# Three classical pairs instead of four ahead of the Strassen pairs in both feed-forwards, with the roles of two buffer sets exchanged and another order of work at the hand-over

## The chip, the cores and the metric

One core of a Trainium2 chip runs the whole kernel. The metric is the device time of one execution in microseconds; lower is better.

## The reference

Two layers of an encoder on x of shape (1, 512, 1024), all in float32. Layer 0 mixes tokens with gated linear attention, layer 1 with chunked softmax attention; behind each mixer stands a residual LayerNorm, then a SwiGLU feed-forward and a second residual LayerNorm. The change touches only the feed-forward, which runs once in each layer:

```python
FFN_HIDDEN = -(-8 * D_MODEL // (3 * 256)) * 256        # 2816
def swiglu(x, w_in, w_out):
    gate, up = jnp.split(x @ w_in, 2, axis=-1)
    return (jax.nn.silu(gate) * up) @ w_out
...
        h = layer_norm(DEEPNORM_ALPHA * h + swiglu(h, ffn_w_in[i], ffn_w_out[i]), ln_g[i, 1], ln_b[i, 1])
```

## The kernel before

Every large product is made in three TensorE matmuls: both operands are held as a high part (rounded to fp32r by ScalarE, "hi") and the rest (made by VectorE or GpSimd as value minus high part, "lo"), and `three` adds hi x hi, hi x lo and lo x hi in PSUM. Weights come as a stream of slabs of 128 x 1024, two to a DMA, into two raw buffers (`raw`). Each raw buffer is loaded again when both parts of its two slabs are made (the wait of SyncE before `load_pair`).

The hidden width of 2816 is 22 chunks of 128 columns. A chunk takes a pair of slabs, one of gate and one of up weights. The first four pairs (`PLAIN = 4`) are classical: 8 blocks of 128 rows for gate and for up, all 512 tokens, 48 matmuls of 512 columns (in pairs 0 and 1 the tokens are taken in two halves, because the LayerNorm ahead delivers them so). Behind them, 18 pairs (`FAST`) are made by a Strassen scheme: gate weights over up weights times early over late tokens is a 2 x 2 block product, made in 7 half-size products of 12 matmuls of 256 columns each instead of 8. `pair` of TensorE has them in order: product 1 (a11), 2 (s3), 3 (s2), 4 (a12), 5 (s1), 6 (a22), 7 (s4). Products 1, 3, 5 and 7 are added in one bank, `out_a`, whose state ScalarE copies out on the way: `copy_p1` behind product 1, `copy_u2` behind 3, `copy_u4` behind 5, `gate_late` behind 7. TensorE may begin product 3 only after `copy_p1`, 5 only after `copy_u2`, 7 only after `copy_u4`.

What the other engines do for pair (i, j), which is Strassen pair 2i + j, in program order on each in-order engine:

- VectorE, one pair ahead: the sums of weights `sums_31` and `sums_24`, and the low parts `form_plain_low`, `form_s32_low`, `form_s1_low`, `form_s4_low`. Behind the products it adds banks to the copies (`gate_of_early`, `u3`, `up_of_late`, `up_of_early`) and multiplies gate by up (`hidden_early`, `hidden_late`).
- ScalarE, one pair ahead: the high parts `form_plain_high`, `form_s32_high`, `form_s1_high`, `form_a22_high`, `form_s4_high`; then the copies and the two Silu (`gate_early`, `gate_late`).
- GpSimd: the low parts of classical slabs (`split_lo`), and of one block of each Strassen pair (`form_a22_low`, 128 x 512), which it starts when its high part is there.

Sums of x are needed once for a feed-forward: `sum_x` makes t1, t2, t3 and t4; ScalarE and VectorE split them. The split of t4 is written over tokens that classical products read, so it waits for the last of these. Its VectorE half (line 1316, "split of t4" below) stands in the queue of VectorE ahead of all forms of pair (0, 1), and its ScalarE half (line 679) ahead of the copies of pair (0, 0). Product 6 of the first pair waits for it.

In the head of a feed-forward, `plain_prod(c)` of VectorE multiplies Silu of gate (`gate(c)` of ScalarE) by the bank of up for classical pair c. `w_s32`, `w_s4` are two sets of buffers for the weight sums, `gate_s` and `prod` hold the copies, two halves each.

Of the kernel before, what the change touches and what calls it, by code (L numbers as in the profile page):

```python
# [82 lines left out]
PLAIN = 4  # L83
# [24 lines left out]
def build_program(nc, a):  # L108
    ctx = ExitStack()
    with ctx:  # L110
# [89 lines left out]
        def halves_at(name, shape, hi, lo):  # L200
# [6 lines left out]
        w_s32 = [halves_at("w_s32_0", [P, 2, HALF], region + 76 * KB, region + 44 * KB),  # L207
                 halves_at("w_s32_1", [P, 2, HALF], region + 68 * KB, gb_at)]
        w_s4 = [halves_at("w_s4_0", [P, HALF], region + 80 * KB, region + 82 * KB),
                halves_at("w_s4_1", [P, HALF], region + 72 * KB, region + 74 * KB)]  # L210
# [198 lines left out]
        def blocks_of(n0, j):  # L409

            slot = (n0 + 2 * j) % RING
            return slot, slot + 1, (n0 // 2 + j) % RAWS
# [59 lines left out]
        def _(act):  # L472
# [94 lines left out]
            def feed_forward(f, n0):  # L567
                banks = SUM_BANKS[f]

                def gate(c):  # L570
                    act.wait_ge(slab_done, n0 + 2 * c + 1)
                    if c >= 2:
                        act.wait_ge(prod_done[f], c - 1)
                    nc.scalar.activation(gate_s[:, c % 2, :], bank[GATE_BANKS[f][c % 2]][:, :], ACT.Silu).then_inc(silu_done[f], 1)
# [109 lines left out]
                with act.Fori(2, FAST // 2 - 1) as i:  # L684
                    pair(i, 0, False, False)
                    pair(i, 1, False, False)
                pair(FAST // 2 - 1, 0, False, False)
                pair(FAST // 2 - 1, 1, False, False, True)
                hidden_high(f, 2)
                gate_late(FAST // 2 - 1, 1, False)  # L690
# [262 lines left out]
        def _(pool):  # L953
# [30 lines left out]
            def feed_forward(f, n0):  # L984
# [93 lines left out]
        def _(dve):  # L1078
# [80 lines left out]
            def sum_x(f, ln):  # L1159
# [31 lines left out]
            def feed_forward(f, n0):  # L1191
                banks = SUM_BANKS[f]

                def plain_prod(c):
                    dve.wait_ge(slab_done, n0 + 2 * c + 2)
                    dve.wait_ge(silu_done[f], c + 1)
                    nc.vector.tensor_tensor(act_a[:, c, :], gate_s[:, c % 2, :], bank[UP_BANKS[f][c % 2]][:, :],
# [77 lines left out]
                def pair(i, j, begun, last=False):  # L1275
# [31 lines left out]
                plain_prod(2)  # L1307
# [6 lines left out]
                plain_prod(3)  # L1314
# [3 lines left out]
                pair(0, 0, False)  # L1318
                pair(0, 1, True)
                with dve.Fori(1, FAST // 2 - 1) as i:  # L1320
                    pair(i, 0, True)
                    pair(i, 1, True)
                pair(FAST // 2 - 1, 0, True)
                pair(FAST // 2 - 1, 1, True, True)
                up_of_late(FAST // 2 - 1, 1)
                up_of_early(FAST // 2 - 1, 1)
                hidden_early(FAST // 2 - 1, 1)
                hidden_low(f, 2)
                hidden_late(FAST // 2 - 1, 1)
# [272 lines left out]
        def _(pe):  # L1602
# [121 lines left out]
            def feed_forward(f, n0, ln):  # L1724
# [14 lines left out]
                for c in range(RING):  # L1739
# [415 lines left out]
```

## Time and profile before

| what | value |
|---|---|
| median of 3 runs | 1172.85 us (1171.49 to 1173.0) |
| the profiled execution's own time | 1171.48 us |
| its span | 1169.8 us |
| PE busy | 1154.0 us, 99% of the span |
| DVE / ACT / POOL busy | 696.7 / 528.0 / 419.9 us |
| share of the chain that ended last on PE | 93% |

The profile is one execution. PE is TensorE's matmuls, DVE is VectorE, ACT is ScalarE, POOL is GpSimd. In a timeline, a row has the start in us from the start of the span, the duration in us, engine, line, operation, output and inputs. In square brackets stands how long the engine was idle before it and what ended that; a row without brackets followed on its predecessor, or nearly. Durations of neighbours overlap a little, since an engine issues the next instruction before the last is drained, so the cost of an instruction in a full queue is the distance of two starts.

### The profile page before, as it was taken

To read this page: it belongs to the slowest core of one execution; us is meant where nothing else is said; L and a number is where in the kernel's file an instruction comes from. 1 tells how busy PE (TensorE), PEld (TensorE's weight loads), DVE (VectorE), ACT (ScalarE), POOL (GpSimd) and SP (SyncE) were. 2 spreads that over 40 slices of the span, in tenths; PEclk is the share of its full clock that TensorE was granted. 3 is DMA by queue.
4 is the path that set the end of the run, shared out by engine and by line. 5 is a ranking of instruction groups with operands and counts; after the bars stand their busy time and mean duration, and the time that the engine had idled before them with its cause. 6 is when DMAs were issued, how large, how long until landed. Compare 5 with 4: busy or idle time off the path is not lost.

```text
span 1169.8 us, 18906 instructions
## 1 busy us (share of the span) xinstructions
PE 1154.0 (99%) x6958; PEld 1019.0 (87%) x6958; DVE 696.7 (60%) x1173; ACT 528.0 (45%) x918; POOL 419.9 (36%) x247
## 2 busy tenths in 40 slices
PE   8999999999999999999999999999999999999997
PEld 6887888989999998888887777778999999998885
DVE  4070163788888874443504676736888888854435
ACT  4345244245555554332415666662455555553222
POOL 2538426041111115446245343472311111144441
PEclk9999999999999999999999999999999999999999
DMA  6433314142233333325032212142223333333211
GB/s 219 154 152 108 108 37 144 49 149 97 104 108 108 108 108 144 107 74 180 19 108 73 90 46 90 46 145 72 69 76 109 108 108 108 108 120 121 84 72 72
DMA packets 21976, 119.89 MB, mean 102 GB/s; under 512 B 2448, under 2 KB 6672, under 8 KB 8992
## 3 DMA queue, kind: packets, MB, share of 16 engines
q1 hardware_dynamic: 15440, 104.96, 25.5%
q10 hardware_dynamic: 6480, 14.17, 3.5%
q8 instruction: 37, 0.61, 0.2%
q14 instruction: 19, 0.16, 0.0%
HBM read 117.02 MB, written 5.24 MB: 105 GB/s over the span
## 4 chain that ended last, share of the span: by engine, by line
PE 93%; DVE 3%; ACT 2%; POOL 1%; DMA 1%; issue 1%; ACTq 0%; DVEq 0%; POOLq 0%
PE bank L1605 28%; PE bank L1607 28%; PE bank L1606 28%; PE bank L1996 2%; PE bank L1981 2%; PE bank L1667 1%; DVE s_g_c L1384 1%; DMA s_x_t<-x_t 1%; PE bank L2017 1%; PE bank L2016 1%; PE bank L1865 1%; PE bank L1858 0%; PE bank L1873 0%; POOL s_g_rg L1026 0%; POOL s_w_lo L970 0%
## 5 line engine op out<-in xcount | busy, mean ns | idle before, releaser
L970 POOL TENSOR_TENSOR s_w_lo<-s_raw,s_w_hi 128x1024 fp32r<-128x1024 f32 x108 | 266.3, 2476 | 307.5 <-ACT s_w_hi L497 307.5
L1605 PE MATMUL bank<-s_t_hi,s_w_hi 128*128 128x256 f32 (+1 forms) x832 | 265.4, 319 | 0.7 <-POOL s_w_lo L970 0.7
L1607 PE MATMUL bank<-s_t_hi,s_w_lo 128*128 128x256 f32 (+1 forms) x832 | 263.1, 316 | 0.0
L1606 PE MATMUL bank<-s_t_lo,s_w_hi 128*128 128x256 f32 (+1 forms) x832 | 262.7, 316 | 0.0
L497 ACT ACTIVATE s_w_hi<-s_raw 128x1024 fp32r<-128x1024 f32 x111 | 116.3, 1059 | 225.0 <-PE bank L1607 200.2
L989 POOL TENSOR_TENSOR s_w_lo<-s_raw,s_w_hi 128x512 fp32r<-128x512 f32 x36 | 64.3, 1785 | 305.1 <-ACT s_w_hi L597 305.1
L1607 PEld LDWEIGHTS bank<-s_t_hi,s_w_lo 128*128 128x128 f32 x832 | 158.6, 191 | 10.6
L1605 PEld LDWEIGHTS bank<-s_t_hi,s_w_hi 128*128 128x128 f32 x832 | 158.7, 191 | 10.2 <-POOL s_w_lo L970 1.1
L1606 PEld LDWEIGHTS bank<-s_t_lo,s_w_hi 128*128 128x128 f32 x832 | 158.8, 191 | 9.3
L1188 DVE TENSOR_TENSOR s_a_lo<-s_act_a,s_a_hi 128x512 fp32r<-128x512 f32 x44 | 84.7, 1938 | 108.7 <-ACT s_a_hi L565 108.5
L1605 PE MATMUL bank<-s_w_hi,s_a_hi 128*128 128x512 f32 x352 | 137.2, 390 | 0.0
L1606 PE MATMUL bank<-s_w_lo,s_a_hi 128*128 128x512 f32 x352 | 137.0, 389 | 0.0
L1607 PE MATMUL bank<-s_w_hi,s_a_lo 128*128 128x512 f32 x352 | 137.0, 389 | 0.0
L1605 PE MATMUL bank<-s_t_hi,s_w_s_hi 128*128 128x256 f32 x432 | 122.4, 283 | 0.0
L1607 PE MATMUL bank<-s_t_hi,s_w_s_lo 128*128 128x256 f32 x432 | 122.3, 283 | 0.0
L1606 PE MATMUL bank<-s_t_lo,s_w_s_hi 128*128 128x256 f32 x432 | 122.2, 283 | 0.0
L1605 PE MATMUL bank<-s_w_hi,s_t_hi 128*128 128x512 f32 x288 | 113.9, 395 | 3.3 <-DVE s_t_lo L1350 1.4
L1607 PE MATMUL bank<-s_w_hi,s_t_lo 128*128 128x512 f32 x288 | 112.3, 390 | 0.0
L1606 PE MATMUL bank<-s_w_lo,s_t_hi 128*128 128x512 f32 x288 | 112.1, 389 | 0.0
L1605 PEld LDWEIGHTS bank<-s_t_hi,s_w_s_hi 128*128 128x128 f32 x432 | 82.9, 192 | 0.1
L1606 PEld LDWEIGHTS bank<-s_t_lo,s_w_s_hi 128*128 128x128 f32 x432 | 82.9, 192 | 0.0
L1607 PEld LDWEIGHTS bank<-s_t_hi,s_w_s_lo 128*128 128x128 f32 x432 | 82.9, 192 | 0.0
(200 smaller groups left out, 2052.8 us busy)
## 6 DMA issues: line engine op xcount, KB each, us to landing
s_raw<-stream SPq DMA_DIRECT2D x97, 1024.0 KB, 4.7
s_ln_gb<-ln_gb ACTq DMA_DIRECT2D x4, 1024.0 KB, 5.9
bias_rows<-rel_bias ACTq DMA_DIRECT2D x1, 3072.0 KB, 12.7
s_h<-x ACTq DMA_DIRECT2D x1, 2048.0 KB, 12.5
s_r_b<-bias_rows ACTq DMA_DIRECT2D x16, 128.0 KB, 2.4
s_x_t<-x_t ACTq DMA_DIRECT2D x3, 512.0 KB, 12.5
out<-s_h SPq DMA_DIRECT2D x3, 512.0 KB, 2.6
s_x_t<-x_t ACTq DMA_DIRECT2D x2, 256.0 KB, 5.8
```

The lines of the kernel that those rows point to most:

```text
L497: nc.scalar.activation(w_parts(n, slice(0, SLAB))[0], raw[:, pair % RAWS, n % 2, :], ACT.Copy).then_inc(hi_done, 2 if n == 1 else 1)
L970: nc.gpsimd.tensor_tensor(lo, raw[:, place // 2 % RAWS, n % 2, :], hi.bitcast(F32), ALU.subtract).then_inc(lo_done, 2 if n == 1 else 1)
L989: nc.gpsimd.tensor_tensor(w_lo[:, up_at, HALF:], raw[:, slot, 1, HALF:], w_hi[:, up_at, HALF:].bitcast(F32), ALU.subtract).then_inc(lo_don ...
L1188: nc.vector.tensor_tensor(a_lo[:, k, :], act_a[:, k, :], a_hi[k % HI_RING][:, :].bitcast(F32), ALU.subtract).then_inc(a_lo_done[f], 1)
L1384: nc.vector.tensor_tensor_scan(g_c[:, hd, :], keep[:, :], g_c[:, hd, :], 0.0, ALU.mult, ALU.add).then_inc(cum_done, 1)
L1605: nc.tensor.matmul(out, l_hi, r_hi, start=start, stop=False, skip_group_check=skip)
L1606: nc.tensor.matmul(out, l_hi, r_lo, start=False, stop=False, skip_group_check=skip)
L1607: return nc.tensor.matmul(out, l_lo, r_hi, start=False, stop=stop, skip_group_check=skip)
L1667: last = nc.tensor.transpose(bank[banks[t][half]][:, k * P:(k + 1) * P], src[:, t, (4 * half + k) * P:(4 * half + k + 1) * P], ident[:, :])
L1865: last = nc.tensor.matmul(bank[GLA_O_BANKS[t][hd // 2]][:, (hd % 2) * GLA_DV:(hd % 2 + 1) * GLA_DV], g_am[:, t % 2, hd * P:(hd + 1) * P], ...
L1981: last = nc.tensor.matmul(bank[2 + hd][:, keys], qk[q][rows, toks], qk[k][rows, keys], start=(i == 0), stop=(i == 2))
L1996: last = nc.tensor.transpose(bank[4 + hd][:, at * P:(at + 1) * P], r_p[:, s % 4, j * P:(j + 1) * P], ident[:, :])
```

## The change

`PLAIN` goes from 4 to 3, and `FAST` so from 18 to 19: nine iterations of two pairs and one more pair, (9, 0), at the end, which is now the last with j = 0. The classical pair that goes is one of the two made whole (48 matmuls of 512 columns). The two sets of `w_s32` and `w_s4` exchange their places, and the classical gates use the two halves of `gate_s` in the other order. On VectorE the second half of t4's sum becomes `add_x4` and moves from ahead of `plain_prod(0)` to behind the forms of pair (0, 0); `plain_prod(2)` is the last classical product. The first Strassen pair gets functions of its own: on ScalarE `copy_p1` and then the split of t4, on VectorE the sums of pair (0, 1) first, then `gate_of_early`, `u3`, and `up_of_late` between the low parts.

The comments that name an engine are added here.

```diff
-PLAIN = 4
+PLAIN = 3
...
-        w_s32 = [halves_at("w_s32_0", [P, 2, HALF], region + 76 * KB, region + 44 * KB),
-                 halves_at("w_s32_1", [P, 2, HALF], region + 68 * KB, gb_at)]
+        w_s32 = [halves_at("w_s32_0", [P, 2, HALF], region + 68 * KB, gb_at),
+                 halves_at("w_s32_1", [P, 2, HALF], region + 76 * KB, region + 44 * KB)]
...
-            slot = (n0 + 2 * j) % RING
-            return slot, slot + 1, (n0 // 2 + j) % RAWS
+            slot = (n0 + 2 * (PLAIN + j)) % RING
+            return slot, slot + 1, (n0 // 2 + PLAIN + j) % RAWS
...
                 def pair(i, j, start, before_start, last=False):     # ScalarE
                     i_next, j_next = (i, 1) if j == 0 else (i + 1, 0)
-                    if before_start is not None:
-                        gate_late(i if j else i - 1, 1 - j, before_start)
+                    gate_late(i if j else i - 1, 1 - j, before_start)
...
-                    if before_start is None:
-                        copy_u2(i, j)
                     form_s32_high(i_next, j_next)
                     form_s1_high(i_next, j_next)
                     form_a22_high(i_next, j_next)
-                    if before_start is not None:
-                        copy_u2(i, j)
+                    copy_u2(i, j)
                     form_s4_high(i_next, j_next)
                     gate_early(i, j)
                     copy_u4(i, j, start)
+
+                def first_pair():                                    # ScalarE
+                    copy_p1(0, 0, True)
+                    act.wait_ge(slab_done, n0 + 2 * PLAIN)
+                    act.wait_ge(x_summed[f], 4)
+                    nc.scalar.activation(t_hi[:, 0:KD // 2, LATE_TOKS], t4_sum[:, :, :], ACT.Copy).then_inc(x_sum_hi[f], 1)
+                    copy_u2(0, 0)
+                    form_plain_high(0, 1)
+                    copy_u4(0, 0, True)
+                    form_s32_high(0, 1)
+                    form_s1_high(0, 1)
+                    form_a22_high(0, 1)
+                    form_s4_high(0, 1)
+                    gate_early(0, 0)
 
                 gate(0)
                 split_hi(n0 + RING)
                 split_hi(n0 + RING + 1)
                 x_sums_high()
                 gate(1)
-                split_hi(n0 + RING + 2)
-                split_hi(n0 + RING + 3)
-                gate(2)
                 form_plain_high(0, 0)
...
                 form_s4_high(0, 0)
-                gate(3)
-                act.wait_ge(slab_done, n0 + 2 * PLAIN)
-                act.wait_ge(x_summed[f], 4)
-                nc.scalar.activation(t_hi[:, 0:KD // 2, LATE_TOKS], t4_sum[:, :, :], ACT.Copy).then_inc(x_sum_hi[f], 1)
-                pair(0, 0, True, None)
+                gate(2)
+                first_pair()
                 pair(0, 1, True, True)
...
+                def first_pair():                                    # VectorE
+                    sums_31(0, 1)
+                    sums_24(0, 1)
+                    gate_of_early(0, 0)
+                    u3(0, 0)
+                    form_plain_low(0, 1)
+                    up_of_late(0, 0)
+                    form_s32_low(0, 1)
+                    form_s1_low(0, 1)
+                    form_s4_low(0, 1)
...
                 plain_prod(1)
-                plain_prod(2)
                 sums_31(0, 0)
                 sums_24(0, 0)
                 form_plain_low(0, 0)
                 form_s32_low(0, 0)
                 form_s1_low(0, 0)
                 form_s4_low(0, 0)
-                plain_prod(3)
+                add_x4(f)
+                plain_prod(2)
                 dve.wait_ge(x_sum_hi[f], 4)
                 nc.vector.tensor_tensor(t_lo[:, 0:KD // 2, LATE_TOKS], t4_sum[:, :, :], t_hi[:, 0:KD // 2, LATE_TOKS].bitcast(F32),
                                         ALU.subtract).then_inc(x_sum_lo[f], 1)
-                pair(0, 0, False)
-                pair(0, 1, True)
+                first_pair()
+                pair(0, 1, late_made=True)
...
-                for c in range(RING):                                # TensorE
+                for c in range(2 * PLAIN - RING):
                     pe.wait_ge(lo_done, n0 + RING + c + 1)
...
                 with pe.Fori(1, FAST // 2) as i:
                     pair(i, 0, False)
                     pair(i, 1, False)
+                pair(FAST // 2, 0, False)
```

With `late_made`, VectorE's `pair` leaves out its `up_of_late`, which `first_pair` has made. GpSimd gets one `form_a22_low` more behind its loop and two `split_lo` fewer in each head.

## Rows read from the trace of the kernel before

**Rows 1.** The page, part 1: busy time and share of the span by engine.
```profile
PE 1154.0 (99%) x6958; PEld 1019.0 (87%) x6958; DVE 696.7 (60%) x1173; ACT 528.0 (45%) x918; POOL 419.9 (36%) x247
```

**Rows 2.** Waits of PE over the whole run: total, times, longest (us).
```profile
PE bank L1605 <- DVE s_t_lo L1350: 1.4, 1, 1.4
```

**Rows 3.** Timeline of PE: start, duration, instruction; the head of feed-forward 0.
```profile
242.38 0.40 PE L1605 MATMUL bank<-s_t_hi,s_w_hi 128*128 128x512 f32 x1
...
264.17 0.28 PE L1605 MATMUL bank<-s_t_hi,s_w_hi 128*128 128x256 f32 x1
...
274.31 0.28 PE L1605 MATMUL bank<-s_t_hi,s_w_hi 128*128 128x256 f32 x1
...
280.07 0.28 PE L1605 MATMUL bank<-s_t_hi,s_w_hi 128*128 128x256 f32 x1
...
284.39 0.28 PE L1605 MATMUL bank<-s_t_hi,s_w_hi 128*128 128x256 f32 x1
```

**Rows 4.** Timeline of DVE, same head; 862.00 is the second head.
```profile
241.90 3.31 DVE L1181 TENSOR_TENSOR s_t_sum<-s_t_sum,s_t_lo 128x1024 f32<-128x1024 f32 x1
...
254.09 0.69 DVE L1204 TENSOR_TENSOR s_w_s_sum<-s_raw 128x512 f32<-128x512 f32 x1
...
257.88 1.22 DVE L1227 TENSOR_TENSOR s_w_s_lo<-s_w_s_sum,s_w_s_hi 128x1024 fp32r<-128x1024 f32 x1
...
259.02 1.79 DVE L1233 TENSOR_TENSOR s_w_lo<-s_s_sum,s_w_hi 128x512 fp32r<-128x512 f32 x1
...
260.73 0.68 DVE L1238 TENSOR_TENSOR s_w_s_lo<-s_w_s_sum,s_w_s_hi 128x512 fp32r<-128x512 f32 x1
...
265.46 1.22 DVE L1316 TENSOR_TENSOR s_t_lo<-s_t_sum,s_t_hi 128x1024 fp32r<-128x1024 f32 x1 [0.41 <-ACT s_t_hi L679]
...
272.19 1.12 DVE L1233 TENSOR_TENSOR s_w_lo<-s_s_sum,s_w_hi 128x512 fp32r<-128x512 f32 x1
...
273.24 0.68 DVE L1238 TENSOR_TENSOR s_w_s_lo<-s_w_s_sum,s_w_s_hi 128x512 fp32r<-128x512 f32 x1
...
276.57 0.68 DVE L1212 TENSOR_TENSOR s_w_s_sum<-s_s_sum,s_raw 128x512 f32<-128x512 f32 x1
...
862.00 1.23 DVE L1316 TENSOR_TENSOR s_t_lo<-s_t_sum,s_t_hi 128x1024 fp32r<-128x1024 f32 x1 [0.41 <-ACT s_t_hi L679]
```

**Rows 5.** The page, part 6: loads of weights; count, KB each, median us to landing.
```profile
s_raw<-stream SPq DMA_DIRECT2D x97, 1024.0 KB, 4.7
```

**Rows 6.** Timeline of ACT, same head.
```profile
256.14 1.06 ACT L589 ACTIVATE s_w_s_hi<-s_w_s_sum 128x1024 fp32r<-128x1024 f32 x1 [1.23 <-DVE s_w_s_sum L1212]
...
264.37 1.06 ACT L679 ACTIVATE s_t_hi<-s_t_sum 128x1024 fp32r<-128x1024 f32 x1 [4.84 <-PE bank L1607]
...
268.68 0.38 ACT L613 ACTIVATE s_gate_s<-bank 128x256 f32<-128x256 f32 x1 [2.04 <-PE bank L1607]
...
277.28 1.06 ACT L589 ACTIVATE s_w_s_hi<-s_w_s_sum 128x1024 fp32r<-128x1024 f32 x1 [0.95 <-DVE s_w_s_sum L1212]
...
279.29 0.36 ACT L613 ACTIVATE s_gate_s<-bank 128x256 f32<-128x256 f32 x1
...
279.55 0.62 ACT L601 ACTIVATE s_w_s_hi<-s_w_s_sum 128x512 fp32r<-128x512 f32 x1
```

**Rows 7.** Timeline of POOL, same head: what it writes for the first two Strassen pairs.
```profile
258.37 1.88 POOL L989 TENSOR_TENSOR s_w_lo<-s_raw,s_w_hi 128x512 fp32r<-128x512 f32 x1 [10.90 <-ACT s_w_hi L597]
...
271.18 1.59 POOL L989 TENSOR_TENSOR s_w_lo<-s_raw,s_w_hi 128x512 fp32r<-128x512 f32 x1 [10.92 <-ACT s_w_hi L597]
```

**Rows 8.** Timeline of DVE and PE where PE waits for line 1350.
```profile
13.30 1.22 DVE L1350 TENSOR_TENSOR s_t_lo<-s_x_t,s_t_hi 128x1024 fp32r<-128x1024 f32 x1 [0.29 <-ACT s_t_hi L715]
...
14.98 0.39 PE L1606 MATMUL bank<-s_w_lo,s_t_hi 128*128 128x512 f32 x1
```

**Rows 9.** Windows: length, then busy us of PE, PEld, DVE, ACT, POOL; a later pair.
```profile
284.40:294.50 10.10, 10.10 (x87) 10.10 (x86) 8.32 (x14) 5.48 (x10) 1.80 (x1) 1.00 0.36 127
```

**Rows 10.** The page, part 2: granted TensorE clock in 40 slices, in tenths.
```profile
PEclk9999999999999999999999999999999999999999
```

More of the change, by code:

```diff
@@ L573, in gate @@
                         act.wait_ge(prod_done[f], c - 1)
-                    nc.scalar.activation(gate_s[:, c % 2, :], bank[GATE_BANKS[f][c % 2]][:, :], ACT.Silu).then_inc(silu_done[f], 1)
+                    nc.scalar.activation(gate_s[:, (c + 1) % 2, :], bank[GATE_BANKS[f][c % 2]][:, :], ACT.Silu).then_inc(silu_done[f], 1)
                 def x_sums_high():
@@ L683, in feed_forward @@
                 pair(1, 1, False, False)
-                with act.Fori(2, FAST // 2 - 1) as i:
+                with act.Fori(2, FAST // 2) as i:
                     pair(i, 0, False, False)
                     pair(i, 1, False, False)
-                pair(FAST // 2 - 1, 0, False, False)
-                pair(FAST // 2 - 1, 1, False, False, True)
+                pair(FAST // 2, 0, False, False, True)
                 hidden_high(f, 2)
-                gate_late(FAST // 2 - 1, 1, False)
+                gate_late(FAST // 2, 0, False)
                 for k in range(3, HI_RING):
@@ L998, in feed_forward @@
                     form_a22_low(i, 1)
+                form_a22_low(FAST // 2, 0)
                 for n in range(n0 + 2 * KF, n0 + 2 * KF + RING):
@@ L1180, in sum_x, with add_x4 @@
                 own(nc.vector.tensor_tensor(t4_sum[:, :, :], t_hi[:, KD // 2:, EARLY_TOKS].bitcast(F32), t2[:, :, :], ALU.subtract))
+            def add_x4(f):
                 nc.vector.tensor_tensor(t4_sum[:, :, :], t4_sum[:, :, :], t_lo[:, KD // 2:, EARLY_TOKS].bitcast(F32),
                                         ALU.add).then_inc(x_summed[f], 1)
-                dve.wait_ge(x_summed[f], 4)
             def hidden_low(f, k):
@@ L1196, in plain_prod @@
                     dve.wait_ge(silu_done[f], c + 1)
-                    nc.vector.tensor_tensor(act_a[:, c, :], gate_s[:, c % 2, :], bank[UP_BANKS[f][c % 2]][:, :],
+                    nc.vector.tensor_tensor(act_a[:, c, :], gate_s[:, (c + 1) % 2, :], bank[UP_BANKS[f][c % 2]][:, :],
                                             ALU.mult).then_inc(prod_done[f], 1)
@@ L1273, in hidden_late, with pair @@
                     hidden(i, j, LATE_TOKS, prod[:, bass.ds(j, 1), LATE_TOKS], prod[:, bass.ds(j, 1), EARLY_TOKS], 2)
-                def pair(i, j, begun, last=False):
+                def first_pair():
[8 more added lines that the diff above has]
+                    form_s4_low(0, 1)
+                def pair(i, j, late_made=False, last=False):
                     i_next, j_next = (i, 1) if j == 0 else (i + 1, 0)
                     i_old, j_old = (i, 0) if j == 1 else (i - 1, 1)
-                    if begun:
+                    if not late_made:
                         up_of_late(i_old, j_old)
-                        up_of_early(i_old, j_old)
-                        hidden_early(i_old, j_old)
+                    up_of_early(i_old, j_old)
+                    hidden_early(i_old, j_old)
                     if not last:
                         sums_31(i_next, j_next)
-                    if begun:
-                        hidden_late(i_old, j_old)
+                    hidden_late(i_old, j_old)
                     if last:
@@ L1317, in feed_forward @@
                                         ALU.subtract).then_inc(x_sum_lo[f], 1)
-                pair(0, 0, False)
-                pair(0, 1, True)
[L1320 to L1327, printed above, removed]
+                first_pair()
+                pair(0, 1, late_made=True)
+                with dve.Fori(1, FAST // 2) as i:
+                    pair(i, 0)
+                    pair(i, 1)
+                pair(FAST // 2, 0, last=True)
+                up_of_late(FAST // 2, 0)
+                up_of_early(FAST // 2, 0)
+                hidden_early(FAST // 2, 0)
                 hidden_low(f, 2)
-                hidden_late(FAST // 2 - 1, 1)
+                hidden_late(FAST // 2, 0)
                 for k in range(3, KF):
```

4 lines of the change are left out of this document (2 added, 2 removed).

## The prediction

> **What bounds the kernel now.** I read the shares first. TensorE is busy for 99% of the span [rows 1], no other engine for more than 60%. Then its waits: behind the first matmuls the longest is 1.4 us, at 13 us of the span [rows 2], and none lies in a feed-forward. Then the starts of its matmuls in the head of feed-forward 0 [rows 3]: from 242.38 to 264.17 lie 96 matmuls of 512 columns, (264.17 - 242.38) / 96 = 0.227 us each; from 274.31 to 284.39 the 84 of a Strassen pair, 0.120 us each. Both stretches are free of gaps. So the time is TensorE's queue, and a change is worth what it takes out of that queue less the gaps that it opens. The second head repeats the first: line 1316 runs there at 862.00 after the same idle time of 0.41 as at 265.46 [rows 4]. All terms below count twice.
>
> **What goes out of TensorE's queue.** A classical pair of 48 x 0.227 = 10.90 us is replaced by one more Strassen pair of 84 x 0.120 = 10.08 us [rows 3]. That is -0.82 us per head, -1.64 us in all. The first Strassen pair keeps its 10.14 us (274.31 - 264.17). If nothing waits, this is the whole effect.
>
> **Are the forms of pair (0, 0) there in time?** Let T be the start of product 1 of pair (0, 0); it was 264.17 and becomes 242.38 + 10.90 = 253.28. There is still one classical pair to cover the forms. `add_x4` leaves the front of VectorE, so `plain_prod(0)` starts where line 1181 did, at 241.90. With 1.14 for a 1024-wide instruction (257.88 to 259.02) and 0.6 for a 512-wide one (half of it and the overhead; line 1238 lasts 0.68 with the overlap) [rows 4], the sums begin at 241.90 + 0.6 + 3 x 1.14 + 0.6 = 246.5, the low part of s32 ends 257.88 + 1.22 - 254.09 = 5.0 us later at 251.5, and s4's issue is over at 246.5 + (260.73 + 0.6 - 254.09) = 253.8, T + 0.5. Products 1 and 2 need only the parts up to s32: 1.8 us to spare at T. s1 and s4 are needed at T + 5.8 and T + 8.6. `add_x4` is then over at about T + 0.5 + 1.2 = T + 1.7. So no gap here; I price it at 0, and from the other side at 0.5 us, should the three low parts of the x sums run slower than 1.14.
> The two `split_lo` that go from GpSimd, the exchanged buffers and the halves of `gate_s` change no wait that is last: the buffers' former readers are classical slabs or the LayerNorm, done before 242.38. GpSimd's part of pair (0, 0) ends 1.15 behind the low part of s32, as before (260.25 against 259.10), so at 252.7, T - 0.6; it was T - 3.9. Only then is the raw buffer of pair (1, 0) loaded: 4.7 us [rows 5], landed at T + 4.3 and first wanted at T + 10. Price 0; 0.3 if a load took twice that.
>
> **The split of t4 moves to the back of the first copy.** Before, ScalarE began it at 264.37, T + 0.20 [rows 6], and VectorE's half followed at 265.46, T + 1.29 [rows 4]. Now `copy_p1` stands ahead of it. `copy_u2` in the same pair began at 268.68, ended by a wait for PE [rows 6]: three products are 36 x 0.120 = 4.32, so the answer to PE takes 0.19. `copy_p1` so starts at T + 1.44 + 0.19 = T + 1.63, the next instruction 0.26 later (279.29 to 279.55) [rows 6]: t4's ScalarE half starts at T + 1.89, VectorE's half at T + 1.89 + 1.09 = T + 3.0. VectorE is 1.7 us later than before at this point, and everything that forms pair (0, 1) and begins pair (1, 0) is behind it in the queue. Between 265.46 and 276.57 no row of VectorE has idle time ahead of it to make this up [rows 4].
>
> **What is late next.** I follow the same instructions with their distances of before. `s1_low` of pair (0, 1) was at 272.19, 6.73 behind the split [rows 4]; one `up_of_late` (256 columns, 0.33 by the 512-wide ones) is put ahead of it: T + 10.06, with `s32_low` 1.14 ahead at T + 8.92. GpSimd: `copy_u4` starts at T + 7.20 + 0.19, the high parts follow at T + 7.65, and `form_a22_low` is ready to start 258.37 - 256.14 = 2.23 after that, T + 9.88 [rows 6, 7]. That is inside `s32_low`, just as in pair (0, 0) of before (257.88, 258.37, 259.02): there GpSimd ended 1.15 us after `s32_low` (260.25 against 259.10), `s1_low` ended 0.56 us after GpSimd, and it cost 260.73 - 259.02 = 1.71 us instead of 0.6 [rows 4, 7]. For pair (0, 1) before, two additions from PSUM lay between, and it cost 1.05. They are now ahead of the low parts, so I take 1.71: `s4_low` at T + 11.77, where it was at T + 9.07. `up_of_late` is done already (-0.33), so from here VectorE is 2.37 us late.
> The Trainium skill, page SBUF — State Buffer, section "Who interferes with whom", says that a VectorE instruction with two SBUF inputs and a GpSimd instruction that reads SBUF exclude each other, and that the later one waits for the whole of the first. By that rule `s1_low` would run its full 0.68 behind GpSimd's end; the rows have 0.56 and 0.54. The sum would be 0.1 us larger per head.
> `sums_24` of pair (1, 0) was at 276.57, T + 12.40, and comes at T + 14.77. ScalarE's high part of s32 follows 0.71 later (277.28), T + 15.48, and `copy_u2` of pair (0, 1) is queued behind that and two more high parts: 279.29 - 277.28 = 2.01 later, T + 17.49, ending at T + 17.85 [rows 4, 6]. Behind this copy waits product 5 of pair (0, 1). It started at 280.07 = T + 15.90 [rows 3], when the copy had ended at 279.65, 0.42 us before. After a wait TensorE takes up its pace 14.98 - 0.227 - (13.30 + 1.22) = 0.23 us behind the release [rows 8]: T + 18.08. The gap is 18.08 - 15.90 = 2.2 us.
> Bounds of this gap: with a lag of 0.4 in place of 0.19 at each of the two answers of ScalarE to PE in the chain, 2.6. If GpSimd gets in only after `s1_low`, the extra 0.66 is not paid: 1.5. Below that only if the queue is not as I read it: 0.
> Behind it the delay ends. VectorE needs 8.32 of the 10.1 us of a pair [rows 9], and the gap itself gives it 2.2 us. `copy_u4` of (0, 1), queued behind `form_s4_high` and `gate_early`, is wanted at T + 21.0 and can start at T + 19.7; the first low part of (1, 0) ends near T + 17.4, wanted at T + 22.4. The last pair with j = 0 instead of 1 has the same instructions and waits: 0, or at most a few tenths.
>
> **Sum.** Per head -0.82 + 2.2 = +1.4, twice +2.8 us. The profiled execution becomes 1171.48 + 2.8 = 1174.3; its 1171.48 lies 1.37 under the median of the runs, so I put the same sum on the median: 1172.85 + 2.8 = 1175.6 us, +0.24%.
>
> **Rivals.**
> (1) No gap; the order with the copies first holds TensorE, and only the queue's saving is left: -1.64, 1171.2. For it: the copy had 0.42 to spare, and ScalarE is idle much of the time. Against it: the 1.7 us are larger than this, and VectorE's queue had no idle time between the two points. It decides if VectorE's lag at `sums_24` of (1, 0) stays under 0.2 us. This is the not-slower side.
> (2) The gap without the collision: 1.5 per head, +1.4 in all, 1174.2. GpSimd's start at T + 9.88 is only 0.2 ahead of the end of `s32_low`; a few tenths would turn the order.
> (3) A second gap per head, of about 1 us, because `form_a22_low` or the first forms come late as well: +4.8, 1177.6. Against it: the spare times above.
> (4) The gap lets the clock fall. It would be longer than any wait since 13 us, and the granted clock stands at full in all slices [rows 10]. At 1.2 instead of 2.4 GHz the 36 matmuls left in the pair would cost 4.3 us more, 8.6 in all: 1184.
> The Trainium skill, page TensorE: Matmul & The Clock Gate, section "HAM oscillation — how this bites in real kernels", says that idle gaps between matmuls can halve the clock. No wait here did that; 1.4 us did not.
>
> **How the numbers follow.** The forecast has 0.50, rival (1) 0.15, (2) 0.18, (3) 0.13, (4) 0.04. A measurement of this kernel can tell about 0.2%, 2.35 us, from no change. Slower by more: most of the forecast (0.37; its own range is 1174.6 to 1176.5), (3) and (4): 0.53. Same: the rest of the forecast, (2) and nearly all of (1): 0.43. Faster: 0.04, since -1.64 is within the bound. The range of 1171.0 to 1177.8 holds all but (4) and a little of the others' spread; the runs of before alone spread over 1.5 us.
>
> **What would show it.** Right: one wait of TensorE of about 2.2 us in each head, in front of product 5 of pair (0, 1), released by ScalarE's copy at line 613; that copy behind three high parts; the split of t4 at T + 3.0 on VectorE; `s1_low` of pair (0, 1) of 1.7 us beside a GpSimd row; 10.08 us for each later pair. Wrong: no such wait, or one at T, T + 7.2 or in pair (1, 0), or a granted clock under full.

## The result and the profile after

| | median of all runs | lowest to highest | runs |
|---|---|---|---|
| before | 1171.49 us | 1171.02 to 1173.0 | 6 |
| after | 1176.17 us | 1174.57 to 1178.21 | 6 |

The ratio is 1.0035, with a 95% interval of 1.0025 to 1.0046: the change makes the kernel 4.7 us slower. The forecast of +2.8 us, a ratio of 1.0024, lies just below this interval; the forecast of the time, 1175.6 us, is 0.6 us off. The profiled execution of after took 1175.38 us, 3.90 more than that of before, with a span of 1173.7 us. The functions moved down by 17 lines in `three` (L1605 to L1607 became L1622 to L1624), line 1316 is now 1334, 1227 is 1234, 1233 is 1240, 1238 is 1245, 1212 is 1219, 679 is 664.

The page of after, part 1, against [rows 1]: 72 more matmuls are recorded (each pair exchanged turns 48 into 84), and TensorE's busy time is 1.2 us less, though the span is longer. What came on top is waiting.

```profile
PE 1152.8 (98%) x7030; PEld 1020.9 (87%) x7030; DVE 706.1 (60%) x1199; ACT 533.6 (45%) x932; POOL 410.8 (35%) x245
```

The longest of TensorE's waits in after, with total, times and longest:

```profile
PE bank L1622 <- ACT s_gate_s L613: 4.0, 2, 2.0
```

This is a wait that before did not have: twice 2.0 us, released by ScalarE's copy at line 613. The timeline of TensorE in head 0 of after answers to [rows 3]:

```profile
243.35 0.40 PE L1622 MATMUL bank<-s_t_hi,s_w_hi 128*128 128x512 f32 x1
...
254.25 0.28 PE L1622 MATMUL bank<-s_t_hi,s_w_hi 128*128 128x256 f32 x1
...
264.33 0.28 PE L1622 MATMUL bank<-s_t_hi,s_w_hi 128*128 128x256 f32 x1
...
269.97 0.28 PE L1624 MATMUL bank<-s_t_hi,s_w_lo 128*128 128x256 f32 x1
272.26 0.36 PE L1622 MATMUL bank<-s_t_hi,s_w_hi 128*128 128x256 f32 x1 [2.01 <-ACT s_gate_s L613]
...
276.65 0.28 PE L1622 MATMUL bank<-s_t_hi,s_w_hi 128*128 128x256 f32 x1
...
286.73 0.28 PE L1622 MATMUL bank<-s_t_hi,s_w_hi 128*128 128x256 f32 x1
```

Three stretches are to be read. Classical pair to T: 254.25 - 243.35 = 10.90. Pair (0, 0): 10.08. Pair (0, 1): 276.65 - 264.33 = 12.32 in place of 10.08; behind its product 4 TensorE starts nothing for 272.26 - 269.97 = 2.29 us, 2.17 more than its pace. Pair (1, 0): 10.08 again. The second feed-forward shows the same at 868.07. From the first of these classical matmuls to the end of the last pair a feed-forward took 203.29 us before (242.38 to 445.67, and 838.92 to 1042.21) and takes 204.66 and 204.65 now (to 448.01 and 1046.10): 1.36 us more each.

The other engines in the same head, T = 254.25; VectorE, against [rows 4]:

```profile
257.25 1.23 DVE L1334 TENSOR_TENSOR s_t_lo<-s_t_sum,s_t_hi 128x1024 fp32r<-128x1024 f32 x1 [0.72 <-ACT s_t_hi L664]
...
263.18 1.22 DVE L1234 TENSOR_TENSOR s_w_s_lo<-s_w_s_sum,s_w_s_hi 128x1024 fp32r<-128x1024 f32 x1
264.31 1.79 DVE L1240 TENSOR_TENSOR s_w_lo<-s_s_sum,s_w_hi 128x512 fp32r<-128x512 f32 x1
266.03 0.68 DVE L1245 TENSOR_TENSOR s_w_s_lo<-s_w_s_sum,s_w_s_hi 128x512 fp32r<-128x512 f32 x1
...
269.03 0.69 DVE L1219 TENSOR_TENSOR s_w_s_sum<-s_s_sum,s_raw 128x512 f32<-128x512 f32 x1
```

ScalarE, against [rows 6]:

```profile
255.89 0.38 ACT L609 ACTIVATE s_gate_s<-bank 128x256 f32<-128x256 f32 x1 [3.25 <-PE bank L1624]
256.17 1.05 ACT L664 ACTIVATE s_t_hi<-s_t_sum 128x1024 fp32r<-128x1024 f32 x1
...
269.75 1.06 ACT L589 ACTIVATE s_w_s_hi<-s_w_s_sum 128x1024 fp32r<-128x1024 f32 x1 [3.40 <-DVE s_w_s_sum L1219]
...
271.75 0.36 ACT L613 ACTIVATE s_gate_s<-bank 128x256 f32<-128x256 f32 x1
```

GpSimd, against [rows 7]:

```profile
264.15 1.41 POOL L993 TENSOR_TENSOR s_w_lo<-s_raw,s_w_hi 128x512 fp32r<-128x512 f32 x1 [10.50 <-ACT s_w_hi L597]
```

The split of t4 stands at T + 3.00 on VectorE. The low part of s1 takes 1.79 us (266.03 - 264.31 = 1.72 to the next instruction) while GpSimd's row runs beside it. `sums_24` follows at T + 14.78. ScalarE's high part of s32 has waited for that (3.40 us idle), and two more high parts stand between it and the copy at T + 17.50. TensorE starts 0.51 us behind the start of this copy.

The two feed-forwards account for 2 x 1.36 = 2.7 of the 3.9 us between the profiles. Of the rest, 0.2 lies between them, and 0.97 us ahead of head 0, where the change touches nothing: one load landed later. ScalarE's wait for it, first in before, then in after:

```profile
192.00 1.06 ACT L497 ACTIVATE s_w_hi<-s_raw 128x1024 fp32r<-128x1024 f32 x1 [2.35 <-DMA s_raw<-stream]
```
```profile
193.03 1.06 ACT L497 ACTIVATE s_w_hi<-s_raw 128x1024 fp32r<-128x1024 f32 x1 [3.41 <-DMA s_raw<-stream]
```

TensorE then waited for GpSimd's low part of that slab, which it did not do in before:

```profile
198.96 0.50 PE L1622 MATMUL bank<-s_w_hi,s_t_hi 128*128 128x512 f32 x1 [0.67 <-POOL s_w_lo L974]
```

Such a shift comes and goes between executions: head 0 begins between 241.70 and 244.26 in the nine profiles taken after the change was made, in versions that don't differ up to there. So lengths of feed-forwards are compared below, and medians of many runs.

### The profile page after: what moved, and what is told of

Read it like the earlier page. It is cut to its first block, busy times and chain, and to the rows that moved or that the text cites. A ratio compares the mean times of both kernels' runs of the same rounds, so it can differ in the third digit from the quotient of the medians.

```text
span 1173.7 us, 19196 instructions
## 1 busy us (share of the span) xinstructions
PE 1152.8 (98%) x7030; PEld 1020.9 (87%) x7030; DVE 706.1 (60%) x1199; ACT 533.6 (45%) x932; POOL 410.8 (35%) x245
## 4 chain that ended last, share of the span: by engine, by line
PE 86%; DVE 5%; ACT 3%; POOL 2%; issue 1%; DMA 1%; ACTq 0%; DVEq 0%; POOLq 0%; SPq 0%
PE bank L1622 27%; PE bank L1624 26%; PE bank L1623 26%; PE bank L2014 2%; PE bank L1999 2%; DVE s_g_c L1401 1%; PE bank L1684 1%; DMA s_x_t<-x_t 1%; PE bank L2035 1%; PE bank L2034 1%; POOL s_early L974 1%; POOL s_w_lo L974 1%; ACT s_g_on L785 1%; DMA s_raw<-stream 0%; DVE s_bn_o L1473 0%
## 5 line engine op out<-in xcount | busy, mean ns | idle before, releaser
L974 POOL TENSOR_TENSOR s_w_lo<-s_raw,s_w_hi 128x1024 fp32r<-128x1024 f32 x104 | 254.1, 2453 | 314.7 <-ACT s_w_hi L497 314.7
L1622 PE MATMUL bank<-s_t_hi,s_w_hi 128*128 128x256 f32 (+1 forms) x832 | 262.1, 315 | 4.7 <-ACT s_gate_s L613 4.0
L1624 PE MATMUL bank<-s_t_hi,s_w_lo 128*128 128x256 f32 (+1 forms) x832 | 259.6, 312 | 0.0
L497 ACT ACTIVATE s_w_hi<-s_raw 128x1024 fp32r<-128x1024 f32 x107 | 112.2, 1059 | 224.9 <-PE bank L1624 199.1
L993 POOL TENSOR_TENSOR s_w_lo<-s_raw,s_w_hi 128x512 fp32r<-128x512 f32 x38 | 67.7, 1781 | 317.6 <-ACT s_w_hi L597 317.6
L1622 PEld LDWEIGHTS bank<-s_t_hi,s_w_hi 128*128 128x128 f32 x832 | 158.8, 191 | 13.3 <-DVE s_w_lo L1228 4.4
L1624 PEld LDWEIGHTS bank<-s_t_hi,s_w_lo 128*128 128x128 f32 x832 | 158.7, 191 | 9.3
L1622 PE MATMUL bank<-s_w_hi,s_a_hi 128*128 128x512 f32 x352 | 137.2, 390 | 0.0
L1624 PE MATMUL bank<-s_w_hi,s_a_lo 128*128 128x512 f32 x352 | 137.0, 389 | 0.0
L1622 PE MATMUL bank<-s_t_hi,s_w_s_hi 128*128 128x256 f32 x456 | 129.0, 283 | 0.0
L1623 PE MATMUL bank<-s_t_lo,s_w_s_hi 128*128 128x256 f32 x456 | 129.0, 283 | 0.0
L1624 PE MATMUL bank<-s_t_hi,s_w_s_lo 128*128 128x256 f32 x456 | 129.0, 283 | 0.0
L1622 PE MATMUL bank<-s_w_hi,s_t_hi 128*128 128x512 f32 x288 | 114.0, 396 | 4.2 <-DVE s_t_lo L1367 1.5
L1624 PE MATMUL bank<-s_w_hi,s_t_lo 128*128 128x512 f32 x288 | 112.3, 390 | 0.0
L1622 PEld LDWEIGHTS bank<-s_t_hi,s_w_s_hi 128*128 128x128 f32 x456 | 87.6, 192 | 0.0
L1623 PEld LDWEIGHTS bank<-s_t_lo,s_w_s_hi 128*128 128x128 f32 x456 | 87.6, 192 | 0.0
L1624 PEld LDWEIGHTS bank<-s_t_hi,s_w_s_lo 128*128 128x128 f32 x456 | 87.6, 192 | 0.0
```

What stands on the lines that cost most here:

```text
L497: nc.scalar.activation(w_parts(n, slice(0, SLAB))[0], raw[:, pair % RAWS, n % 2, :], ACT.Copy).then_inc(hi_done, 2 if n == 1 else 1)
L974: nc.gpsimd.tensor_tensor(lo, raw[:, place // 2 % RAWS, n % 2, :], hi.bitcast(F32), ALU.subtract).then_inc(lo_done, 2 if n == 1 else 1)
L993: nc.gpsimd.tensor_tensor(w_lo[:, up_at, HALF:], raw[:, slot, 1, HALF:], w_hi[:, up_at, HALF:].bitcast(F32), ALU.subtract).then_inc(lo_don ...
L1622: nc.tensor.matmul(out, l_hi, r_hi, start=start, stop=False, skip_group_check=skip)
L1623: nc.tensor.matmul(out, l_hi, r_lo, start=False, stop=False, skip_group_check=skip)
L1624: return nc.tensor.matmul(out, l_lo, r_hi, start=False, stop=stop, skip_group_check=skip)
```

## The experiments

Each kernel is the changed one with the edit shown. In the first four, before had a median of 1171.38 us on the same chip (24 runs, 1170.58 to 1172.62), in the last four 1171.56 (15 runs, 1170.62 to 1172.84). A feed-forward's length is taken as above; before has 203.29.

**The changed kernel again.** No edit.

> The changed kernel itself, timed once more beside the kernel before on one chip. Theory A (the two waits of 2.2 us less twice 0.82 are the whole systematic effect, and the 1.1 us more that the changed kernel's profile shows is the scatter of when a load lands, as at 193 us of its span): ratio 1.0024 with an interval that holds it, the waits at product 5 of pair (0, 1) again 2.0 us in the list of waits, twice. Theory R (the changed program has about 1.3 us more that belong to it, somewhere ahead of or behind the heads): ratio 1.0035 or more, and the same 1 us late at about 197 us of the span.

Measured: 1175.34 us (1173.73 to 1177.83, 8 runs), ratio 1.0034 (1.0024 to 1.0045). The waits are the same, but the feed-forwards last 204.65 and 206.13 us: the second is 1.5 us longer than the first. TensorE's timeline behind its second wait of 2 us shows where:

```profile
866.68 0.28 PE L1624 MATMUL bank<-s_t_hi,s_w_lo 128*128 128x256 f32 x1
868.97 0.36 PE L1622 MATMUL bank<-s_t_hi,s_w_hi 128*128 128x256 f32 x1 [2.01 <-ACT s_gate_s L613]
...
870.23 0.29 PE L1623 MATMUL bank<-s_t_lo,s_w_hi 128*128 128x256 f32 x1
870.35 0.39 PE L1624 MATMUL bank<-s_t_hi,s_w_lo 128*128 128x256 f32 x1
870.54 0.41 PE L1622 MATMUL bank<-s_t_hi,s_w_hi 128*128 128x256 f32 x1
870.75 0.41 PE L1623 MATMUL bank<-s_t_lo,s_w_hi 128*128 128x256 f32 x1
...
873.52 0.40 PE L1624 MATMUL bank<-s_t_hi,s_w_s_lo 128*128 128x256 f32 x1
873.74 0.31 PE L1622 MATMUL bank<-s_t_hi,s_w_s_hi 128*128 128x256 f32 x1
873.88 0.28 PE L1623 MATMUL bank<-s_t_lo,s_w_s_hi 128*128 128x256 f32 x1
```

Starts are 0.12 us apart up to 870.35 and 0.213 apart from 870.54 to 873.74, with the same shapes, and TensorE waits for nobody. The windows of this stretch (length, busy time of PE, PEld, DVE, ACT, POOL, then the granted clock as a share of 2.4 GHz, DMA share, GB/s):

```profile
866.80:868.90 2.10, 0.16 (x2) 0.00 (x0) 2.10 (x3) 2.10 (x5) 0.11 (x1) 1.00 0.00 0
868.90:871.90 3.00, 2.93 (x19) 2.96 (x20) 3.00 (x6) 1.25 (x3) 1.68 (x1) 0.74 0.15 16
871.90:873.20 1.30, 1.30 (x8) 1.30 (x8) 0.16 (x1) 0.00 (x0) 0.00 (x0) 0.50 0.60 208
873.20:880.00 6.80, 6.80 (x57) 6.80 (x56) 5.78 (x9) 4.41 (x8) 0.38 (x1) 0.96 0.26 110
```

The granted clock is 1.2 GHz for about 3.4 us (870.4 to 873.8) and then full again: 16 matmuls at 0.213 in place of 0.120, 1.5 us. What went ahead is the wait and 1.4 us of work at full pace. The first wait of this execution, and both waits of the other profile, were not followed by it. So rival (4) happens, at 1.5 us instead of the 4.3 that it was priced at, and not every time. Nor did a fall follow any of the four waits of 1.8 us in the profiles of the last two experiments below, where the granted clock behind them is 1.00.

**`copy_u2` ahead of the high parts in pair (0, 1).**

```diff
                     copy_p1(i, j, start)
+                    if start:
+                        copy_u2(i, j)
...
                     form_a22_high(i_next, j_next)
-                    copy_u2(i, j)
+                    if not start:
+                        copy_u2(i, j)
```

> The changed kernel with one move on ScalarE: in pair (0, 1) copy_u2 comes ahead of the three high parts of pair (1, 0), behind copy_p1. Theory Q (the wait is the order of ScalarE's queue: the copy stands behind high parts that wait for VectorE's sums): no wait at product 5 of pair (0, 1), copy_u2 starts 4.5 us behind the start of that pair. What is late next is copy_u4, behind gate_early, which waits for VectorE's gate_of_early: in the changed kernel that ended 273.04 - 254.25 = T + 18.8, so copy_u4 ends at T + 19.5, product 7 is due at T + 18.7, a wait with restart of 1.0 us at product 7. Per head -0.82 + 1.0 = +0.2: 0.4 us over the kernel before, ratio 1.0003. Rival V (VectorE's results themselves are late, whatever ScalarE's order): product 5 still waits about 2 us, for s1's low part or for another VectorE result, ratio 1.0024 or more.

Measured: 1171.69 us (1170.94 to 1172.63, 10 runs), ratio 1.0003 (0.9994 to 1.0013). The wait for line 613 is gone. A shorter one stands in front of product 7 of pair (0, 1), on the copy that is still behind the high parts:

```profile
PE bank L1625 <- ACT s_prod L621: 1.6, 2, 0.8
```

The feed-forwards last 203.42 and 203.41 us, 0.13 more than before: the 0.82 saved against a gap of 1.07 - 0.12 = 0.95. VectorE is exactly as late as in after here (split of t4 at T + 3.0). Its lateness costs only where a copy is queued behind what waits for it.

**Both copies ahead, in pairs (0, 1) and (1, 0).**

```diff
                     copy_p1(i, j, start)
+                    if before_start:
+                        copy_u2(i, j)
...
-                    copy_u2(i, j)
+                    if not before_start:
+                        copy_u2(i, j)
                     form_s4_high(i_next, j_next)
+                    if before_start:
+                        copy_u4(i, j, start)
                     gate_early(i, j)
-                    copy_u4(i, j, start)
+                    if not before_start:
+                        copy_u4(i, j, start)
```

> The changed kernel with copy_u2 ahead of the high parts and copy_u4 ahead of gate_early, in pairs (0, 1) and (1, 0). Theory Q: no wait of TensorE in either head, VectorE 1.7 us late at the sums for pair (1, 1) and caught up one pair later; only the saving is left, -1.64 us, ratio 0.9986, if the saving of 0.82 per head is right. Theory R (1.3 us more belong to the changed program): -0.3 us, ratio 0.9997. Rival V: waits for VectorE's results appear in pair (1, 0) or (1, 1), ratio over 1.0.

Measured: 1170.13 us (1168.84 to 1172.39, 11 runs), ratio 0.9988 (0.9979 to 0.9997). TensorE waits in neither head; the feed-forwards last 202.42 and 202.41 us, 0.87 less than before. So this version is faster than both kernels (1.2 and 5.2 us by the medians). Its feed-forwards are shorter than those of before by what the prediction gave for a pair exchanged (0.82). On ScalarE the copy now stands ahead of the high part of s32, which still waits for VectorE:

```profile
269.76 0.38 ACT L613 ACTIVATE s_gate_s<-bank 128x256 f32<-128x256 f32 x1 [2.50 <-PE bank L1630]
270.66 1.06 ACT L589 ACTIVATE s_w_s_hi<-s_w_s_sum 128x1024 fp32r<-128x1024 f32 x1 [0.52 <-DVE s_w_s_sum L1225]
```

**Nearly no work for GpSimd in pair (0, 1).** GpSimd makes 8 of the 512 columns of a22's low part for this pair; the other 504 keep old contents.

```diff
-                def form_a22_low(i, j):
+                def form_a22_low(i, j, end=SLAB):
...
-                form_a22_low(0, 1)
+                form_a22_low(0, 1, HALF + 8)
```

> The changed kernel where GpSimd makes only 8 of the 512 columns of the low part of a22 for pair (0, 1); the others keep old data, so part of the computation is left out. It measures the share of the collision between GpSimd and VectorE. By the prediction s1_low (line 1240 of the changed kernel), issued at T + 10.1, costs 0.6 instead of 1.71 to the next instruction, everything behind it comes 1.1 earlier, and the wait at product 5 shrinks from 2.2 to 1.1 with the restart (from 2.0 to 0.9 in the list of waits), 2.2 us less in all. Rival: the collision is hidden by other idle time of VectorE and the wait stays 2.0.

Measured in one execution: 1172.35 us, feed-forwards of 203.56 us each. VectorE's low part of s1, GpSimd's row beside it, and TensorE's wait:

```profile
263.54 0.70 DVE L1240 TENSOR_TENSOR s_w_lo<-s_s_sum,s_w_hi 128x512 fp32r<-128x512 f32 x1
```
```profile
263.37 0.31 POOL L993 TENSOR_TENSOR s_w_lo<-s_raw,s_w_hi 128x8 fp32r<-128x8 f32 x1 [10.51 <-ACT s_w_hi L597]
```
```profile
PE bank L1622 <- ACT s_gate_s L613: 1.8, 2, 0.9
```

The low part of s1 takes 0.70 instead of 1.79 us, and the wait falls by the same 1.1 us. So half of the gap comes from VectorE's low part and GpSimd's row falling on the same time, called the collision here.

**The wait filled with matmuls.** 16 matmuls whose result is thrown away stand in front of product 5's wait.

```diff
                     product(out_e, a12, x_block(1, EARLY_TOKS), True).then_inc(multiplied[f], 1)
+                    if first and j == 1:
+                        for _ in range(FILL):
+                            nc.tensor.matmul(bank[UP_BANKS[f][0]][:, EARLY_TOKS], a12[0][:, 0:P], t_hi[:, 0, EARLY_TOKS],
+                                             start=True, stop=True)
```

> The changed kernel with 16 matmuls of 256 columns more, whose output in bank 2 nobody reads, ahead of TensorE's wait for product 5 of pair (0, 1): they take 16 x 0.12 = 1.9 us of the 2.2 us in which TensorE waited, and delay nothing. It settles what the 1.2 us above my sum are. Theory C (after the wait of 2.2 us the clock sometimes falls to the half for 3.4 us, as in the profile of e1 at 870.4 us, where 16 matmuls ran 0.213 apart instead of 0.120, 1.5 us each time, and the eight runs of e1 stand in three groups near 1174.2, 1175.4 and 1177.6): with TensorE at work no fall, all runs within 2 us of each other, ratio 1.0024 (+2.8 us). Theory R (1.2 us more belong to the changed program, or to loads that land late): ratio 1.0034 as in e1, and the same scatter of 4 us.

Measured: 1174.37 us (1173.7 to 1176.09, 11 runs), ratio 1.0026 (1.0017 to 1.0035). The row of the filling, and product 5 behind it at the time at which it came in after (2.17 us behind the fill's start):

```profile
269.11 2.08 PE L1802 MATMUL bank<-s_t_hi,s_w_hi 128*128 128x256 f32 x16
271.28 0.35 PE L1623 MATMUL bank<-s_t_hi,s_w_hi 128*128 128x256 f32 x1
```

The feed-forwards last 204.65 and 204.66 us, as in after, so the work needed is as late as ever. But the median is 1.0 us under that of after again, and the runs spread over 2.4 us instead of 4.1. The two ratios alone don't settle it: their intervals (1.0017 to 1.0035 here, 1.0024 to 1.0045 there) overlap, and the two were measured on different chips, each beside its own runs of before. The clocks say more. Every run's mean granted clock was 0.998 or 0.999 here, as in all 39 runs of before in these experiments. In the 14 runs of the changed kernel it was 0.998 in five (mean time 1174.5 us), 0.997 in seven (1176.1) and 0.996 in two (1178.0). 3.4 us at half clock in 1173 are 0.0014 of the mean. The mean has another part that costs nothing: in every profile the clock is also at half for the last 3.0 to 5.4 us of the span, when TensorE has finished. In before:

```profile
1166.81:1169.70 2.89, 0.00 (x0) 0.00 (x0) 0.50 (x1) 0.00 (x0) 0.00 (x0) 0.50 0.48 181
```

This end takes 0.0013 to 0.0023 from the mean, as an estimate from the ten profiles. With it an execution without a fall should show 0.998 or 0.999 and one with a fall 0.996 or 0.997. So nine of the 14 runs probably had a fall, and none of the 11 with the wait filled. This ties the fall to the idle array and not to the late data. It doesn't explain all of the scatter: two of the 11 runs took 1175.7 and 1176.1 us at 0.998 and 0.999. Nor does 0.996 tell one fall from two.

**Copies first in pair (0, 1) alone.** The edit of the third experiment with `start` in place of `before_start`.

> As e3, but the copies come first in pair (0, 1) alone and pair (1, 0) keeps its order. Theory Q (VectorE is 1.7 us late, and the lag becomes a wait wherever a copy stands behind high parts of the next pair): no wait in pair (0, 1), and the lag comes out one pair later: in pair (1, 0) sums_31 stands 1.7 us behind the start of the pair, copy_u2 ends 6.35 us behind it, product 5 is due at 5.76: with the restart a wait of 0.8 us. Time about 0.8 x 2 - 1.64 = 0 against the kernel before. Rival (the lag is gone by then): no wait at all, as in e3.

Measured in one execution: 1172.05 us, feed-forwards of 203.21 and 203.23 us. The wait moves one pair on, to product 5 of pair (1, 0), 0.70 us over the pace:

```profile
PE bank L1628 <- ACT s_gate_s L613: 1.1, 2, 0.6
```

So VectorE's lateness is not used up inside pair (0, 1). Without a gap that hands it time, it reaches the copies of the next pair too; with both pairs reordered, in the third experiment, no wait is left.

**The split of t4 ahead of the first copy, as in before.**

```diff
-                    copy_p1(0, 0, True)
                     act.wait_ge(slab_done, n0 + 2 * PLAIN)
...
                     nc.scalar.activation(t_hi[:, 0:KD // 2, LATE_TOKS], t4_sum[:, :, :], ACT.Copy).then_inc(x_sum_hi[f], 1)
+                    copy_p1(0, 0, True)
```

> The changed kernel with ScalarE's half of the split of t4 ahead of copy_p1(0, 0), as before the change, and not behind it. add_x4 ends at T + 1.7, so ScalarE's half starts there and not at T + 0.2, VectorE's half comes at T + 2.8 instead of T + 3.0, and copy_p1 ends at T + 3.0, where product 3 is due at T + 2.9: a new wait of 0.36 us with the restart at product 3 of pair (0, 0). My theory: the collision with GpSimd stays and the wait at product 5 of pair (0, 1) is 2.0 us; 2.4 us per head instead of 2.2. Rival (by my prediction's words, the copy ahead of the split costs 1.7 us): the wait at product 5 falls to about 0.5 us.

Measured in one execution: 1175.45 us, feed-forwards of 204.86 us, with one more gap of 0.27 us at product 3 of (0, 0). VectorE, ScalarE's half of the split, and the wait (T = 253.92):

```profile
254.38 1.21 DVE L1189 TENSOR_TENSOR s_t_sum<-s_t_sum,s_t_lo 128x1024 f32<-128x1024 f32 x1
...
256.77 1.22 DVE L1334 TENSOR_TENSOR s_t_lo<-s_t_sum,s_t_hi 128x1024 fp32r<-128x1024 f32 x1 [0.59 <-ACT s_t_hi L663]
...
264.19 0.69 DVE L1240 TENSOR_TENSOR s_w_lo<-s_s_sum,s_w_hi 128x512 fp32r<-128x512 f32 x1
264.79 1.79 DVE L1245 TENSOR_TENSOR s_w_s_lo<-s_w_s_sum,s_w_s_hi 128x512 fp32r<-128x512 f32 x1
```
```profile
255.68 1.06 ACT L663 ACTIVATE s_t_hi<-s_t_sum 128x1024 fp32r<-128x1024 f32 x1 [3.39 <-DVE s_t_sum L1189]
```
```profile
PE bank L1622 <- ACT s_gate_s L613: 3.7, 2, 1.8
```

Undoing this step brings VectorE's half forward only to T + 2.85. ScalarE's half no longer waits for the copy, but for `add_x4` (line 1189), which VectorE begins at 254.38, behind all low parts of pair (0, 0); so it starts at T + 1.76 where it was at T + 1.92. The low part of s1 gets through in 0.69, and the low part of s4 pays 1.79 in its place.

**The same, and `add_x4` back to the front of VectorE.**

```diff
                 plain_prod(0)
+                add_x4(f)
...
                 form_s4_low(0, 0)
-                add_x4(f)
                 plain_prod(2)
```

> As e7, and add_x4 comes straight behind plain_prod(0), so t4's sum is there in time. ScalarE's half starts at T + 0.2 as before the change. VectorE's half waits for plain_prod(2) behind the forms, T + 2.2, 0.8 earlier than in the changed kernel. But the low part of s32 of pair (0, 1) waits for ScalarE, whose high part stands behind copy_u4 at T + 7.4 and ends at T + 8.7: VectorE keeps 0.2 of the 0.8. Theory (ScalarE's queue behind copy_u4 binds as well): a wait of 2.0 us at product 5 of pair (0, 1), none at product 3. Rival (VectorE's lag alone sets the wait): 1.4 us.

Measured in one execution: 1173.36 us, feed-forwards of 204.48 and 204.49 us. VectorE, ScalarE, and the wait:

```profile
254.81 1.21 DVE L1334 TENSOR_TENSOR s_t_lo<-s_t_sum,s_t_hi 128x1024 fp32r<-128x1024 f32 x1
...
261.37 1.22 DVE L1234 TENSOR_TENSOR s_w_s_lo<-s_w_s_sum,s_w_s_hi 128x1024 fp32r<-128x1024 f32 x1 [0.52 <-ACT s_w_s_hi L589]
262.51 0.68 DVE L1240 TENSOR_TENSOR s_w_lo<-s_s_sum,s_w_hi 128x512 fp32r<-128x512 f32 x1
263.11 1.79 DVE L1245 TENSOR_TENSOR s_w_s_lo<-s_w_s_sum,s_w_s_hi 128x512 fp32r<-128x512 f32 x1
```
```profile
260.00 0.38 ACT L621 ACTIVATE s_prod<-bank 128x256 f32<-128x256 f32 x1 [1.55 <-PE bank L1624]
260.28 1.05 ACT L589 ACTIVATE s_w_s_hi<-s_w_s_sum 128x1024 fp32r<-128x1024 f32 x1
```
```profile
PE bank L1622 <- ACT s_gate_s L613: 3.7, 2, 1.8
```

The split is at T + 2.2 (T = 252.61), 0.8 earlier than in after, and yet the wait is 1.8. VectorE now waits 0.52 us for ScalarE's high part of s32, which is queued behind a copy that waits for PE (line 621), and meets GpSimd's row again with s4's low part. In this execution earlier work on VectorE alone gained only 0.17 us per head while ScalarE's queue holds copies and high parts in this order.

## Why the prediction came out as it did

**The queue's saving** was -0.82 per head. It measured 10.90 (classical) against 10.08: right. The version without waits has -0.87, 0.05 more, because pair (0, 0) did not keep its 10.14 us: it took 10.08 like the others.

**Forms of pair (0, 0) in time.** No wait at T or in pair (0, 0); its pair took 10.08 us: right.

**The chain behind the split of t4** was right at every link. Forecast and measured, each behind T: split 3.0 and 3.00; low part of s32 8.92 and 8.93; low part of s1 10.06 and 10.06; low part of s4 11.77 and 11.78; `sums_24` 14.77 and 14.78; copy 17.49 and 17.50; product 5 18.08 and 18.01; gap 2.2 and 2.17. The way to this was to keep the distances between instructions as measured in before and to move only the head of the queue. What the chain blames is confirmed link by link: take the collision away and 1.1 of the wait's 2.0 us goes; move the copy and the whole wait goes. The reading that the split's place is the cause was too narrow, however: with the split put back (seventh and eighth experiment) the gap stays, since `add_x4` now comes late on VectorE, and with that put back too ScalarE's copies hold the high parts to their own times. Rival (2), that a few tenths dodge the collision, is half right: in those two experiments the order did turn, but then the next instruction with two SBUF inputs paid the same 1.1 us. Its price of 1.5 us per head for a gap without the collision was too high: the 1.05 us taken from pair (0, 1) of before holds a part of a collision, too (that row lasts 1.12 us and not 0.68 [rows 4]), and the fourth experiment left a gap of 1.07.

The Trainium skill, page SBUF — State Buffer, section "Who interferes with whom", has the later of the two wait for all of the earlier one. The trace agrees that one waits: the low part of s1 ended 0.54 us behind GpSimd's row (264.31 + 1.79 against 264.15 + 1.41), where it takes 0.68 alone. So 0.14 us of it lay beside GpSimd's row, much as in the rows of before (0.56 and 0.54); how far GpSimd's rows can be trusted to a tenth is not shown.

**Second gap** (rival 3): none in after, but the sixth experiment shows it waiting behind the first, at 0.7 us.

**The sum.** +1.4 per head against +1.36; +2.8 against 2.7 for both. Of the median's difference of 4.7 us (4.0 in the second comparison) this leaves 1.2 to 2.0. The mis-sized term is rival (4): the forecast had the gap leave the clock alone (chance of a fall 0.04), and said that a fall would cost 4.3 us per head, for all 36 matmuls left in the pair. The one fall that a profile shows lasted 3.4 us only and cost 1.5, and the mean clocks point to a fall in nine of the 14 runs. With the wait filled the ratio is 1.0026 instead of 1.0034, 2.8 us, which is the forecast sum, though the intervals overlap. That the whole 1.2 to 2.0 us is the clock's is not shown; a part can be scatter of the loads. The error in reasoning was to treat the clock as a question of yes or no with one length: the longest wait of before behind its first matmul was 1.4 us and said nothing of 2.2, and no row gave the time at the lower clock. The prediction also read too much into [rows 10]: a 9 there means 90% or more of a slice of 29 us, which 3.4 us at half clock leave at 0.94. The page of the second profile has forty times 9 like that of before, in spite of its fall. The Trainium skill, page TensorE: Matmul & The Clock Gate, section "HAM oscillation — how this bites in real kernels", says that gaps in TensorE's work can halve its clock. The second profile agrees, with 0.50 behind one of its waits of 2.0 us; the other three such waits of the two profiles, with no fall behind them, show that it need not.

The predicted 1175.6 us lies near the 1176.17 measured partly by luck: it started from a median of before of 1172.85, of three runs, and six runs gave 1171.49. The offset of 1.4 us in the starting point covered most of what the sum left out.

What stays open is how often the clock falls behind such a wait. The mean clocks suggest a fall in over half of the executions, one of two profiles shows one fall and the other none, and nothing here tells why one wait of 2.0 us is followed by it and the next is not. That the fastest version has no such fall in its heads was seen in one profile; one of its 11 runs, the slowest, had a mean clock of 0.997.

## What to carry to other kernels

To forecast a reordering, keep the measured distances between the instructions of each in-order queue, move the one whose release changes, and follow the delay from queue to queue until something that TensorE needs stands behind it. Where a short instruction that frees the bottleneck stands behind one that waits for a late engine, put it ahead; that was worth 5.2 us against the changed kernel here (1.2 against before), while moving the late engine's work earlier was worth at most 0.2 per head. A new wait on TensorE can cost more than its length, so compare the granted clock behind it in several executions.

## What was not expected of the hardware

Behind a wait of 2.01 us TensorE worked 1.4 us at full pace, then at a granted clock of 0.50 for 3.4 us, starts 0.213 us apart instead of 0.120, and then at full again, without any further idle time. In another execution of the same program the same wait had no such effect.

A GpSimd row that starts while VectorE is still in an instruction with two SBUF inputs delays the next such instruction of VectorE, or the one behind that. In two profiles a difference of 0.16 us decided which. Started 0.25 us ahead of the end of s32's low part (264.15 against 263.18 + 1.22 in after), GpSimd came next: its row is 1.41 us long, and s1's low part paid. Started 0.09 ahead of that end (262.50 against 261.37 + 1.22 in the last experiment; its row is 1.84 us long), it let s1's low part through as well, and s4's paid. In both cases the last 1.15 us of its row run from the end of a VectorE instruction (264.40 to 265.56, 263.19 to 264.34).
